# Attention weights times values in high and low parts, two query blocks at a time

## The chip, the core and the metric

The kernel runs on one core of a Trainium2 chip. The metric is the device time of one execution in microseconds; the median of repeated runs is compared. The core has a matrix engine, TensorE (PE in the rows; PEld is its load of the stationary operand), three engines for elementwise work, VectorE (DVE), ScalarE (ACT) and GpSimd (POOL), and SyncE (SP), which issues DMAs. SBUF is the working memory of 128 partitions, PSUM the memory that TensorE writes, in banks of 512 fp32 columns.

## The reference

One layer of a hybrid block over 1024 prompt tokens and 8 decode tokens of width 1024: differential attention with 8 heads and a gated linear recurrence with 8 heads side by side, then a convolutional feed-forward part. The change touches the attention of the prompt alone, and of it the last product:

```python
s = jnp.einsum('bqhcd,bkhcd->bhcqk', qi, k).astype(F32) * scale
s = jnp.where(kpos[None, :] <= qpos[:, None], s, -jnp.inf)
p = diff_probs(s, lam)        # softmax(s)[c=0] - lam * softmax(s)[c=1]
return jnp.einsum('bhqk,bkhv->bqhv', p.astype(v.dtype), v)
```

Queries go in 8 blocks of 128; block i sees the keys of blocks 0 to i. Everything is fp32.

## The kernel before

The work is laid out by hand: each engine has its own program, and semaphores (`Sig`) order them. The stages are a norm stage, the heads stage, a gates stage and the tail with the feed-forward part. The change is in `heads_stage`, which takes the first half of the span. There a loop over the heads h = 0 to 7 does three things at once: the attention of head h, its recurrence, and the large projections of the inputs (`piece(h, n)`, 21 pieces of 24 products in a head, helper `product` at L170). A piece multiplies high and low parts of weights and of activations: three products of type float32r (high by high, high by low, low by high) for each of 8 contraction tiles, 344 columns wide. Plain fp32 products are also used; in the trace each of those is two MATMUL records, each float32r product is one.

The attention of a head goes through eight query blocks i = 0 to 7 (in the texts: block 0 to 7). For a block, in the order of the data:

- `scores_of(h, i)` on TensorE (L1038): queries times keys into PSUM (`h_S`).
- `maxima(h, i)` on VectorE (L1332 to L1336): mask, row maxima.
- two exponentials on ScalarE (L903) into `E` (`h_a_E`), with their sums.
- `weigh(h, i)` on VectorE (L1342 to L1347): the weights, which raises `weighed`.
- the transposes on TensorE (L1090), i + 1 of them, into the PSUM tile `Xf` (`h_X`), which raises `turned`.
- a copy on ScalarE from `Xf` to `PT` in SBUF (L929), which raises `pt_ready`.
- `values(i, n)` on TensorE (L1067): i + 1 plain fp32 products of 128 columns, `vtok` (the values, tokens on partitions, copied from PSUM at L911) by `PT`, summed in a bank of `G` beside the bank of the next piece; then `read_values(i)` on ScalarE (L897) copies the bank to `oraw`.

TensorE's own program in block i is: scores of block i + 1 (for i + 1 below 4), one piece (i below 4) or two pieces, `values(i - 1)`, in blocks 1 and 2 of heads 1 to 7 a sum matmul for the norm of the recurrence of the head before (`o_sum`, L1049), the transposes of block i, then the scores of block i + 1 (for i + 1 from 4 on). After block 7 come eight transposes of another input, the piece `FILL_PIECE`, `values(7)`, and then the eight chunks of the recurrence, each with a piece among its products. ScalarE's program in blocks 1 and 2 takes the sum's reciprocal root (`o_norm`, L887 and L889) ahead of its copy of the transposes, and VectorE applies it (L1418, L1422) ahead of the next `weigh`.

## Time and profile before

| | us |
|---|---|
| median of 3 runs | 2320.13 |
| lowest and highest | 2319.94 and 2320.91 |
| span of the profiled execution | 2317.6 |
| TensorE busy in it | 2283.8 |
| VectorE busy | 1433.6 |
| ScalarE busy | 1046.8 |
| GpSimd busy | 805.3 |

The span runs from the first to the last instruction of one profiled execution; a run's time holds a little more, what lies around it. A record of a matmul is drawn from its start to the modelled end of its last result, and the next one starts before that end. So the distance from one start to the next tells what a matmul costs, and the length of a record does not. The granted clock of TensorE was 0.997 of full speed (2.4 GHz) over the span. A time in the timeline is counted from the start of the span.

### The profile page before, as it was taken

How to read it: one execution, taken by the hardware profiler on the slowest of the kernel's cores; microseconds unless marked ns; L12 is line 12 of the kernel's file. 1: busy time of each engine (PE TensorE's matmuls, PEld its weight loads, DVE VectorE, ACT ScalarE, POOL GpSimd, SP SyncE). 2: the span in 40 equal slices, each digit the busy share in tenths (PEclk: the TensorE clock that was granted, in tenths of full speed). 3: DMA queues.
4: the chain of work that ended last, by engine and by line, in shares of the span. 5: the costliest groups of instructions: out<-in, count | busy, mean ns of one | idle time of the engine just before them, and what ended most of it. 6: DMA issues, size and time to landing. Idle time of an engine off the chain costs nothing. (4 is left out here: it accounts for less than half of the span.)

```text
span 2317.6 us, 46133 instructions
## 1 busy us (share of the span) xinstructions
PE 2283.8 (99%) x18425; PEld 2153.4 (93%) x18425; DVE 1433.6 (62%) x2594; ACT 1046.8 (45%) x2114; POOL 805.3 (35%) x1019
## 2 busy tenths in 40 slices
PE   7999999999999999999999999999999999999999
PEld 5898989989898989899888999999999999999999
DVE  5667676777676776765787324337546545555557
ACT  6656656556566656564333321125333333332331
POOL 1143342626252434424444124442222323222222
PEclk9999999999999999999999999999999999999999
DMA  7213121222312131211899413111111111111113
GB/s 299 92 47 103 41 87 59 73 77 57 102 54 95 49 101 49 92 46 53 326 346 347 159 61 104 46 48 51 46 46 46 46 46 46 54 43 51 46 46 99
DMA packets 75057, 213.19 MB, mean 92 GB/s; under 512 B 15579, under 2 KB 23643, under 8 KB 74843
## 3 DMA queue, kind: packets, MB, share of 16 engines
q1 hardware_dynamic: 73690, 206.05, 26.6%
q10 hardware_dynamic: 1152, 4.19, 0.4%
q8 instruction: 146, 2.39, 0.4%
q14 instruction: 69, 0.56, 0.1%
HBM read 175.49 MB, written 26.26 MB: 87 GB/s over the span
## 5 line engine op out<-in xcount | busy, mean ns | idle before, releaser
L170 PE MATMUL h_G<-xn_hi,h_w_hi 128*128 128x344 f32 x1368 | 457.7, 335 | 0.2 <-ACT h_d_oraw L897 0.2
L170 PE MATMUL h_G<-xn_hi,h_w_lo 128*128 128x344 f32 x1368 | 437.1, 319 | 0.0
L170 PE MATMUL h_G<-xn_lo,h_w_hi 128*128 128x344 f32 x1368 | 436.5, 319 | 0.0
L2419 POOL TENSOR_TENSOR h_w_lo<-h_w_raw,h_w_hi 128x1024 fp32r<-128x1024 f32 x87 | 215.7, 2480 | 488.8 <-DVE f_y L2620 208.7
L2341 PE MATMUL t_ps<-hn_hi,h_w_hi 128*128 128x344 f32 x1024 | 327.7, 320 | 0.9 <-issue 0.9
L2341 PE MATMUL t_ps<-hn_lo,h_w_hi 128*128 128x344 f32 x1024 | 327.1, 319 | 0.0
L2341 PE MATMUL t_ps<-hn_hi,h_w_lo 128*128 128x344 f32 x1024 | 327.0, 319 | 0.0
L1167 POOL TENSOR_TENSOR h_w_lo<-h_w_raw,h_w_hi 128x1024 fp32r<-128x1024 f32 x58 | 149.2, 2572 | 432.6 <-ACT h_w_hi L764 365.0
L170 PEld LDWEIGHTS h_G<-xn_hi,h_w_hi 128*128 128x128 f32 x1368 | 258.4, 189 | 32.5 <-issue 21.5
L170 PEld LDWEIGHTS h_G<-xn_lo,h_w_hi 128*128 128x128 f32 x1368 | 257.1, 188 | 4.4 <-issue 0.2
L170 PEld LDWEIGHTS h_G<-xn_hi,h_w_lo 128*128 128x128 f32 x1368 | 257.1, 188 | 0.0
L2199 ACT ACTIVATE f_u<-t_ps 128x344 f32<-128x344 f32 x132 | 59.9, 459 | 336.5 <-PE t_ps L2341 335.5
L2149 ACT ACTIVATE h_w_hi<-h_w_raw 128x1024 fp32r<-128x1024 f32 x87 | 91.5, 1053 | 266.5 <-PE t_ps L170 256.5
L2341 PEld LDWEIGHTS t_ps<-hn_hi,h_w_hi 128*128 128x128 f32 x1024 | 192.3, 188 | 1.4 <-issue 1.4
L2341 PEld LDWEIGHTS t_ps<-hn_hi,h_w_lo 128*128 128x128 f32 x1024 | 192.5, 188 | 0.0
L2341 PEld LDWEIGHTS t_ps<-hn_lo,h_w_hi 128*128 128x128 f32 x1024 | 192.3, 188 | 0.0
L2505 DVE SCALAR_TENSOR_TENSOR x<-t_ps,keep_mod,x 128x344 f32<-128x344 f32 (+1 forms) x288 | 149.5, 564 | 68.4 <-PE t_ps L170 67.6
L2613 DVE TENSOR_SCALAR f_y<-f_old,keep_vec 128x8 f32<-128x8 f32 x44 | 16.2, 369 | 259.8 <-ACT f_u L2199 259.8
L170 PE MATMUL t_ps<-f_act_hi,h_w_hi 128*128 128x344 f32 x528 | 169.8, 322 | 0.0
L170 PE MATMUL t_ps<-f_act_hi,h_w_lo 128*128 128x344 f32 x528 | 169.0, 320 | 0.0
L170 PE MATMUL t_ps<-f_act_lo,h_w_hi 128*128 128x344 f32 x528 | 168.7, 320 | 0.0
L903 ACT ACTIVATE h_a_E<-h_S,h_d_sm 128x256 f32<-128x256 f32 (+7 forms) x128 | 93.6, 738 | 115.1 <-DVE h_d_sm L1336 115.1
(403 smaller groups left out, 5510.3 us busy)
## 6 DMA issues: line engine op xcount, KB each, us to landing
h_w_raw<-in_w_in SPq DMA_DIRECT2D x72, 512.0 KB, 3.8
h_w_raw<-in_w_ffn SPq DMA_DIRECT2D x66, 512.0 KB, 3.6
h_d_ada_w<-in_w_ada SPq DMA_DIRECT2D x32, 512.0 KB, 4.3
g_kp<-in_cache_k SPq DMA_DIRECT2D x32, 512.0 KB, 7.1
g_vp<-in_cache_v SPq DMA_DIRECT2D x32, 512.0 KB, 5.6
h_w_raw<-in_w_mix SPq DMA_DIRECT2D x24, 512.0 KB, 3.6
x<-in_xT SPq DMA_DIRECT2D x16, 516.0 KB, 7.5
n_ada_w<-in_w_ada SPq DMA_DIRECT2D x16, 512.0 KB, 13.8
```

The costliest lines, as they stand in the source:

```text
L170: ins = eng.matmul(out, w[:, k * P:(k + 1) * P], x[:, k, columns], start=(k == 0 and n == 0), stop=(k == n_k - 1 and n == 2))
L903: ins = act.activation(E[:, m, 0:nk], SP_[:, :, :].rearrange("p a b -> p (a b)")[:, 512 * score_bank(i, m):512 * score_bank(i, m) + nk], A ...
L1167: pool.tensor_tensor(wlo[w][:, :], raw[r][:, :], whi[w][:, :].bitcast(F32), ALU.subtract).then_inc(lo_done.sem, 1)
L2149: act.activation(whi[buf(n)][:, :], raw[n % 2][:, :], ACT.Copy).then_inc(w_hi.sem, 1)
L2199: act.activation(u[s][:, 2 + j * TH:2 + (j + 1) * TH], ffn_bank(t, 0, j), ACT.Copy).then_inc(up_free.sem, 1)
L2341: ins = pe.matmul(ffn_bank(t, 0, j), wp[w][:, k * P:(k + 1) * P], xp[:, k, cols(j)], start=(k == 0 and q == 0), stop=(k == KT - 1 and q == 2))
L2419: pool.tensor_tensor(wlo[buf(n)][:, :], raw[n % 2][:, :], whi[buf(n)][:, :].bitcast(F32), ALU.subtract).then_inc(w_lo.sem, 1)
L2505: ins = dve.scalar_tensor_tensor(out=xt[:, a0:a0 + n], in0=bank[:, 0:n], scalar=gain[:, 0:1], in1=xt[:, a0:a0 + n], op0=ALU.mult, op1=ALU.add)
L2613: ch(dve.tensor_scalar(ys[:, T:NT], st[0], w[0], w[3], ALU.mult, ALU.add))
```

## The change

The values and the transposed weights are each kept as a high part (float32r, rounded on the copy out of PSUM by ScalarE) and a low part (the difference of PSUM and high part, a subtraction on VectorE). `values(j, n)` now treats the two query blocks 2j and 2j + 1 together: for each of 2j + 2 key blocks three float32r products, high values by high weights, high by low, low by high, 256 columns wide; the last key block is seen by the second query block only, and its three are 128 wide. It is called in blocks 2, 4 and 6 and after `FILL_PIECE`, and one copy of 256 columns reads its bank. `low_values` (one subtraction) and `low_weights` (one or two) are new in VectorE's program. The transposes of a block now wait until high and low weights of the block before have been taken from `Xf`. Buffers change places to make room: `pt_hi` lies over the buffers of the rotation, part of which moves to the place of `E`; the low values lie over the second buffer of the adaptive weights, so its load now waits in SyncE's queue for the last products (`pv_done`), ahead of `turn_piece(h, 1)`.

```diff
         qT, kT, vT = (mem(n, [P, NT]) for n in ("qT", "kT", "vT"))
-        vtok = mem("vtok", [P, T])
+        v_at = mem.off
+        v_hi = mem("vtok_hi", [P, T], F32R)
         kk, fc, qh, ib, og = (mem(n, [P, NT]) for n in ("kk", "fc", "qh", "ib", "og"))
         ibtok = mem("ibtok", [P, T])
         AT, kht, St, subg = mem("AT", [P, P]), mem("kht", [P, P]), mem("St", [P, P]), mem("subg", [P, 1])
...
         LK = [mem(f"LK{i}", [P, LEVELS, P]) for i in range(2)]
-        LQ = [mem(f"LQ{i}", [P, LEVELS + 1, P]) for i in range(2)]
+        LQ = [mem("LQ0", [P, LEVELS + 1, P])]
+        pt_lo = [None, Memory(nc, "h_lq", mem.off)("pt_low1", [P, T], F32R)]
+        LQ.append(mem("LQ1", [P, LEVELS + 1, P]))
         braw = mem("braw", [P, T])
         ex = [mem(f"ex{i}", [P, TH]) for i in range(2)]
         PT = Memory(nc, "h_c", R3 + WIDE)("PT", [P, T])
+        v_first = Memory(nc, "h_vt", v_at)("vtok_first", [P, T])
+        pt_lo[0] = Memory(nc, "h_pt", R3 + WIDE)("pt_low0", [P, T], F32R)
         mem = Memory(nc, "h_d", R3 + WIDE + ROW, early["lmask_at"])
-        rg = [mem(f"rg{i}", [P, TH]) for i in range(2)]
-        rt = [mem(f"rt{i}", [P, TH]) for i in range(2)]
-        rows = Memory(nc, "h_rows", mem.off)("rows", [H * NS, 2, P])
-        sq = [mem(f"sq{i}", [P, TH]) for i in range(2)]
+        pt_at = mem.off
+        pt_hi = Memory(nc, "h_turn", pt_at)("pt_high", [P, NB, 2, P], F32R)
+        rest = Memory(nc, "h_rest", R3, R3 + 2 * ROW)
+        rg, rt, sq = ([rest(f"{n}0", [P, TH]), mem(f"{n}1", [P, TH])] for n in ("rg", "rt", "sq"))
+        rows = mem("rows", [H * NS, 2, P])
+        mem.off = pt_at + NB * 2 * P * 4
         oraw = mem("oraw", [P, T])
+        v_lo = Memory(nc, "h_aw", mem.off + KT * P * 4)("vtok_lo", [P, T], F32R)
         aw, av = [mem(f"ada_w{i}", [P, KT * P]) for i in range(2)], [mem(f"ada{i}", [P, P]) for i in range(2)]
         sm = mem("sm", [P, 16])
         dec, neg_mid = mem("dec", [P, NB]), mem("neg_mid", [P, NB])
...
 
-        def value_bank(i):
-
-            return (ATT_PIECES[i + 1][-1] + 1) % 2 if i + 1 < NB else (FILL_PIECE + 1) % 2
+        def value_bank(j):
+
+            return (ATT_PIECES[2 * j + 2][-1] + 1) % 2 if 2 * j + 2 < NB else (FILL_PIECE + 1) % 2
+
+        def pt_low(b):
+
+            at = b % (NB // 2) * 2 * P
+            return pt_lo[b // (NB // 2)][:, at:at + 2 * P]
+
+        def low_half(n, i, blocks):
+
+            return pt_lo[n][:, :].rearrange("p (b q t) -> p b q t", q=2, t=P)[:, 0:blocks, i % 2, :]
 
 
         def sum_bank(h, u):
...
-                        load_ada(h, 1, 0)
                     if t == 4 and h:
                         store_branch(h - 1, 2)
                         store_branch(h - 1, 3)
                     if t == NTL:
                         turn_piece(h, 0)
                     load(t)
+                sp.wait_ge(pv_done.sem, pv_done.at(h, NB // 2))
+                load_ada(h, 1, 0)
                 turn_piece(h, 1)
                 load_ada(h, 2, 14)
...
 
-                def read_values(i):
-                    act.wait_ge(pv_done.sem, pv_done.at(h, i + 1))
-                    if i == 0 and h:
+                def read_values(j):
+                    act.wait_ge(pv_done.sem, pv_done.at(h, j + 1))
+                    if j == 0 and h:
                         act.wait_ge(a_stored.sem, a_stored.at(h, 0))
-                    act.activation(oraw[:, i * P:(i + 1) * P], G[:, value_bank(i), 0:P], ACT.Copy).then_inc(pv_read.sem, 1)
+                    act.activation(oraw[:, 2 * j * P:2 * (j + 1) * P], G[:, value_bank(j), 0:2 * P], ACT.Copy).then_inc(pv_read.sem, 1)
 
                 for i in range(NB):
                     nk = (i + 1) * P
...
-                        act.activation(vtok[:, :], Xf, ACT.Copy).then_inc(v_tok.sem, 1)
+                        act.activation(v_hi[:, :], Xf, ACT.Copy).then_inc(v_high.sem, 1)
                     for n in ATT_PIECES[i]:
                         if n != READ_FIRST:
                             split_next(h, n)
                         piece(h, n)
                         if n == READ_FIRST:
                             split_next(h, n)
-                    if 0 < i:
-                        read_values(i - 1)
+                    if i in (2, 4, 6):
+                        read_values(i // 2 - 1)
                     if i in (1, 2) and h:
                         o_norm(h - 1, i + 1)
                     if i == 4:
...
-                read_values(NB - 1)
+                read_values(NB // 2 - 1)
                 sigmoid(h, len(SIGMOID) - 1)
 
                 for k in range(NB):
...
                 pe.wait_ge(st_ready.sem, st_ready.at(h, 0))
 
-                def values(i, n):
-
-                    pe.wait_ge(pt_ready.sem, pt_ready.at(h, i + 1))
+                def values(j, n):
+
+                    pe.wait_ge(pt_high.sem, pt_high.at(h, 2 * j + 2))
+                    pe.wait_ge(pt_lowed.sem, pt_lowed.at(h, 2 * j + 2))
                     pe.wait_ge(piece_read.sem, piece_read.at(h, n))
-                    for b in range(i + 1):
-                        ins = pe.matmul(G[:, value_bank(i), 0:P], vtok[:, b * P:(b + 1) * P], PT[:, b * P:(b + 1) * P],
-                                        start=(b == 0), stop=(b == i))
+                    for b in range(2 * j + 2):
+                        q = slice(0 if b <= 2 * j else P, 2 * P)
+                        high = pt_hi[:, b, :, :].rearrange("p q t -> p (q t)")[:, q]
+                        low, out, at = pt_low(b)[:, q], G[:, value_bank(j), q], slice(b * P, (b + 1) * P)
+                        pe.matmul(out, v_hi[:, at], high, start=(b == 0), stop=False)
+                        pe.matmul(out, v_hi[:, at], low, start=False, stop=False)
+                        ins = pe.matmul(out, v_lo[:, at], high, start=False, stop=(b == 2 * j + 1))
                     ins.then_inc(pv_done.sem, 1)
 
                 for i in range(NB):
                     if i + 1 < NB // 2:
                         scores_of(h, i + 1)
                     for n in ATT_PIECES[i]:
-                        if n == ATT_PIECES[i][0] and i >= 2:
-                            pe.wait_ge(pv_read.sem, pv_read.at(h, i - 1))
+                        if n == ATT_PIECES[i][0] and i in (3, 5, 7):
+                            pe.wait_ge(pv_read.sem, pv_read.at(h, (i - 1) // 2))
                         piece(h, n)
-                    if 0 < i:
-                        values(i - 1, ATT_PIECES[i][-1])
+                    if i in (2, 4, 6):
+                        values(i // 2 - 1, ATT_PIECES[i][-1])
                     if i in (1, 2) and h:
                         if i == 2:
                             pe.wait_ge(o_rstd.sem, o_rstd.at(h - 1, 3))
@@ -1085,7 +1109,11 @@
                         pe.wait_ge(o_rstd.sem, o_rstd.at(h, 0))
                     pe.wait_ge(weighed.sem, weighed.at(h, i + 1))
                     if i == 0:
-                        pe.wait_ge(v_tok.sem, v_tok.at(h, 1))
+                        pe.wait_ge(v_high.sem, v_high.at(h, 1))
+                        pe.wait_ge(v_low.sem, v_low.at(h, 1))
+                    else:
+                        pe.wait_ge(pt_high.sem, pt_high.at(h, i))
+                        pe.wait_ge(pt_lowed.sem, pt_lowed.at(h, i))
                     for b in range(i + 1):
                         ins = pe.transpose(Xf[:, b * P:(b + 1) * P], E[:, 0, b * P:(b + 1) * P], ident[:, :])
                     ins.then_inc(turned.sem, 1)
...
                         scores_of(h, i + 1)
                 pe.wait_ge(piece_read.sem, piece_read.at(h, 9))
                 turn8(Sf, ib).then_inc(ib_turned.sem, 1)
-                pe.wait_ge(pv_read.sem, pv_read.at(h, NB - 1))
                 piece(h, FILL_PIECE)
-                values(NB - 1, FILL_PIECE)
+                values(NB // 2 - 1, FILL_PIECE)
                 for k in range(NB):
                     ck = slice(k * P, (k + 1) * P)
                     pe.wait_ge(lv_k.sem, lv_k.at(h, k + 1))
...
+
+            def low_values(h):
+
+                dve.wait_ge(v_high.sem, v_high.at(h, 1))
+                if h:
+                    dve.wait_ge(ada_read.sem, ada_read.at(h, 0))
+                dve.tensor_tensor(v_lo[:, :], Xf, v_hi[:, :].bitcast(F32), ALU.subtract).then_inc(v_low.sem, 1)
+
+            def low_weights(h, i):
+
+                dve.wait_ge(pt_high.sem, pt_high.at(h, i + 1))
+                for n in range(1 + i // (NB // 2)):
+                    at = n * NB // 2
+                    blocks = min(NB // 2, i + 1 - at)
+                    ins = dve.tensor_tensor(low_half(n, i, blocks), Xf[:, at * P:(at + blocks) * P].rearrange("p (b t) -> p b t", t=P),
+                                            pt_hi[:, at:at + blocks, i % 2, :].bitcast(F32), ALU.subtract)
+                ins.then_inc(pt_lowed.sem, 1)
...
                 for i in range(NB):
                     weigh(h, i)
+                    if i == 0:
+                        low_values(h)
...
                         o_norm(h - 1, i + 1)
                     if NB // 2 <= i + 1 < NB:
                         maxima(h, i + 1)
+                    low_weights(h, i)
```

TensorE, second head: the end of a piece, the products of block 1 and the transposes of block 2, before. `h_c_PT` are the transposed weights, `h_vtok` the values, `h_d_rstd_o` what the sum matmul sums, `h_a_E` the weights.

```order
L170 MATMUL h_G<-xn_hi,h_w_lo_79 128x344
L1067 MATMUL h_G<-h_c_PT,h_vtok 128x128 [waits h_piece_read,h_pt_ready]
L1067 MATMUL h_G<-h_c_PT,h_vtok 128x128
L1049 MATMUL h_X<-h_d_rstd_o,keep_ones_50 128x512 [waits h_o_squared,h_o_rstd]
L1090 MATMUL h_X<-keep_ident,h_a_E 128x128 [waits h_weighed]
L1090 MATMUL h_X<-keep_ident,h_a_E 128x128 x2
L170 MATMUL h_G<-xn_hi,h_w_hi_78 128x344 [waits h_w_lo_done,h_piece_read,h_w_hi_done,h_pv_read]
```

The same place with the change (`h_turn_pt_high` and `h_pt_pt_low` are the high and low weights, `h_vtok_hi` and `h_aw_vtok_lo` the values):

```order
L170 MATMUL h_G<-xn_hi,h_w_lo_79 128x344
L1090 MATMUL h_G<-h_turn_pt_high,h_vtok_hi 128x256 [waits h_piece_read,h_pt_low,h_pt_high]
L1091 MATMUL h_G<-h_pt_pt_low_827,h_vtok_hi 128x256
L1092 MATMUL h_G<-h_turn_pt_high,h_aw_vtok_lo 128x256
L1090 MATMUL h_G<-h_turn_pt_high,h_vtok_hi 128x128
L1091 MATMUL h_G<-h_pt_pt_low_827,h_vtok_hi 128x128
L1092 MATMUL h_G<-h_turn_pt_high,h_aw_vtok_lo 128x128
L1068 MATMUL h_X<-h_d_rstd_o,keep_ones_50 128x512 [waits h_o_squared,h_o_rstd]
L1118 MATMUL h_X<-keep_ident,h_a_E 128x128 [waits h_pt_low,h_pt_high,h_weighed]
L1118 MATMUL h_X<-keep_ident,h_a_E 128x128 x2
L170 MATMUL h_G<-xn_hi,h_w_hi_78 128x344 [waits h_w_lo_done,h_piece_read,h_w_hi_done,h_pv_read]
```

Two products of 128 columns have become six of up to 256, for blocks 0 and 1 together, and the transposes wait for two more semaphores.

TensorE, second head, the end of block 3's piece and the transposes of block 3, before:

```order
L170 MATMUL h_G<-xn_lo,h_w_hi_78 128x344
L170 MATMUL h_G<-xn_hi,h_w_lo_80 128x344
L1067 MATMUL h_G<-h_c_PT,h_vtok 128x128 [waits h_piece_read,h_pt_ready]
L1067 MATMUL h_G<-h_c_PT,h_vtok 128x128 x2
L1090 MATMUL h_X<-keep_ident,h_a_E 128x128 [waits h_weighed]
L1090 MATMUL h_X<-keep_ident,h_a_E 128x128 x3
L1038 MATMUL h_S<-h_kT,h_qT 128x512
```

and with the change:

```order
L170 MATMUL h_G<-xn_lo,h_w_hi_78 128x344
L170 MATMUL h_G<-xn_hi,h_w_lo_80 128x344
L1118 MATMUL h_X<-keep_ident,h_a_E 128x128 [waits h_pt_low,h_pt_high,h_weighed]
L1118 MATMUL h_X<-keep_ident,h_a_E 128x128 x3
L1057 MATMUL h_S<-h_kT,h_qT 128x512
L1057 MATMUL h_S<-h_kT,h_qT 128x128
```

Nothing stands any more between the piece and the transposes.

VectorE, second head, between the row maxima and the weights of block 3, before (`h_b_braw` and `h_og` are of the norm, L1342 is the reciprocal with which `weigh` starts):

```order
L1363 TENSOR_SCALAR h_fc<-h_b_ex_823,keep_lb 128x344 [waits h_sig_ready]
L1365 TENSOR_SCALAR h_kk<-h_fc 128x344 [waits h_dve_chain]
L1418 SCALAR_TENSOR_TENSOR h_b_braw<-h_b_braw,keep_vec,h_d_rstd_o 128x512 [waits h_o_rstd]
L1422 TENSOR_TENSOR h_b_braw<-h_b_braw,h_og 128x512 [waits h_dve_chain]
L1342 RECIPROCAL h_d_sm<-h_d_sm 128x2 [waits h_exped]
L1344 TENSOR_TENSOR h_d_sm<-h_d_sm,keep_lam 128x1 [waits h_dve_chain]
L1345 TENSOR_SCALAR h_a_E<-h_a_E,h_d_sm 128x512
```

and with the change:

```order
L1407 TENSOR_SCALAR h_fc<-h_b_ex_824,keep_lb 128x344 [waits h_sig_ready]
L1409 TENSOR_SCALAR h_kk<-h_fc 128x344 [waits h_dve_chain]
L1462 SCALAR_TENSOR_TENSOR h_b_braw<-h_b_braw,keep_vec,h_d_rstd_o 128x512 [waits h_o_rstd]
L1466 TENSOR_TENSOR h_b_braw<-h_b_braw,h_og 128x512 [waits h_dve_chain]
L1390 TENSOR_TENSOR h_pt_pt_low_827<-h_X,h_turn_pt_high 128x3x128 [waits h_pt_high]
L1369 RECIPROCAL h_d_sm<-h_d_sm 128x2 [waits h_exped]
L1371 TENSOR_TENSOR h_d_sm<-h_d_sm,keep_lam 128x1 [waits h_dve_chain]
L1372 TENSOR_SCALAR h_a_E<-h_a_E,h_d_sm 128x512
```

The subtraction for the low weights of block 2 (L1390, three blocks of 128) has come in ahead of the reciprocal of block 3.

## Rows read from the trace of the kernel before

**Rows 1.** The page: its first line and busy time by engine

```profile
span 2317.6 us, 46133 instructions
...
PE 2283.8 (99%) x18425; PEld 2153.4 (93%) x18425; DVE 1433.6 (62%) x2594; ACT 1046.8 (45%) x2114; POOL 805.3 (35%) x1019
```

**Rows 2.** Groups of TensorE by line and form: records, busy us, mean ns, idle before

```profile
L1067 PE MATMUL h_G<-h_c_PT,h_vtok 128*128 128x128 f32 x576 | 74.6, 275 | 0.0
```

**Rows 3.** Timeline of TensorE, blocks 2 and 3: start us, length us, instruction, records

```profile
603.25 0.61 PE L1067 MATMUL h_G<-h_c_PT,h_vtok 128*128 128x128 f32 x4
603.70 1.02 PE L1049 MATMUL h_X<-h_d_rstd_o,keep_ones 128*128 128x512 f32 x2
604.56 0.49 PE L1090 MATMUL h_X<-keep_ident,h_a_E 128*128 128x128 f32 x3
604.80 0.41 PE L170 MATMUL h_G<-xn_hi,h_w_hi 128*128 128x344 f32 x1
605.05 0.32 PE L170 MATMUL h_G<-xn_lo,h_w_hi 128*128 128x344 f32 x1
...
608.65 0.83 PE L1067 MATMUL h_G<-h_c_PT,h_vtok 128*128 128x128 f32 x6
609.46 0.66 PE L1090 MATMUL h_X<-keep_ident,h_a_E 128*128 128x128 f32 x4
```

**Rows 4.** Timeline of TensorE at two records of nine columns

```profile
585.05 0.28 PE L1019 MATMUL h_G<-keep_pick,h_d_ada 128*128 128x9 f32 x2
585.19 0.47 PE L1150 MATMUL h_S<-h_AT,h_ibtok 128*128 128x128 f32 x2
585.49 0.39 PE L1152 MATMUL h_S<-h_b_LQ,h_St 128*128 128x128 f32 x2
```

**Rows 5.** Timeline of ScalarE up to the exponentials of block 3

```profile
604.76 0.69 ACT L887 ACTIVATE h_d_rstd_o<-h_X,keep_eps 128x512 f32<-128x512 f32 x1 [0.45 <-PE h_X L1049]
...
606.02 0.47 ACT L929 ACTIVATE h_c_PT<-h_X 128x384 f32<-128x384 f32 x1
606.39 0.68 ACT L903 ACTIVATE h_a_E<-h_S,h_d_sm 128x512 f32<-128x512 f32 x1
...
607.05 0.69 ACT L903 ACTIVATE h_a_E<-h_S,h_d_sm 128x512 f32<-128x512 f32 x1
```

**Rows 6.** Timeline of VectorE up to the weights of block 3

```profile
606.93 0.69 DVE L1422 TENSOR_TENSOR h_b_braw<-h_b_braw,h_og 128x512 f32<-128x512 f32 x1
607.86 0.17 DVE L1342 RECIPROCAL h_d_sm<-h_d_sm 128x2 f32<-128x2 f32 x1 [0.23 <-ACT h_a_E L903]
...
608.65 0.75 DVE L1347 SCALAR_TENSOR_TENSOR h_a_E<-h_a_E,h_d_sm 128x512 f32<-128x512 f32 x1
```

**Rows 7.** Timeline of VectorE: ends of weighing in blocks 5 and 7

```profile
627.45 1.02 DVE L1347 SCALAR_TENSOR_TENSOR h_a_E<-h_a_E,h_d_sm 128x768 f32<-128x768 f32 x1
...
650.49 0.17 DVE L1342 RECIPROCAL h_d_sm<-h_d_sm 128x2 f32<-128x2 f32 x1 [2.37 <-ACT h_a_E L903]
...
651.54 1.28 DVE L1347 SCALAR_TENSOR_TENSOR h_a_E<-h_a_E,h_d_sm 128x1024 f32<-128x1024 f32 x1
```

**Rows 8.** Timeline of TensorE: products and transposes of blocks 5 and 7

```profile
629.68 1.27 PE L1067 MATMUL h_G<-h_c_PT,h_vtok 128*128 128x128 f32 x10
630.79 0.82 PE L1090 MATMUL h_X<-keep_ident,h_a_E 128*128 128x128 f32 x6
...
652.69 1.72 PE L1067 MATMUL h_G<-h_c_PT,h_vtok 128*128 128x128 f32 x14
654.25 1.04 PE L1090 MATMUL h_X<-keep_ident,h_a_E 128*128 128x128 f32 x8
```

**Rows 9.** Timelines: first transposes of two heads, the values' copy, a long product

```profile
465.16 0.27 PE L1090 MATMUL h_X<-keep_ident,h_a_E 128*128 128x128 f32 x1
...
589.29 1.02 ACT L911 ACTIVATE h_vtok<-h_X 128x1024 f32<-128x1024 f32 x1
...
591.99 0.27 PE L1090 MATMUL h_X<-keep_ident,h_a_E 128*128 128x128 f32 x1
...
642.40 1.22 DVE L1445 TENSOR_TENSOR h_fc<-h_fc,h_qh 128x1024 f32<-128x1024 f32 x1
```

More of the change, by code:

```diff
@@ L604, in heads_stage @@
         scores, row_max, exped, weighed = S("scores", 8), S("row_max", 8), S("exped", 8), S("weighed", 8)
-        turned, pt_ready, pv_done, pv_read = S("turned", 8), S("pt_ready", 8), S("pv_done", 8), S("pv_read", 8)
-        v_turned, v_tok = S("v_turned", 1), S("v_tok", 1)
+        turned, pv_done, pv_read = S("turned", 8), S("pv_done", 4), S("pv_read", 4)
+        pt_high, pt_lowed = S("pt_high", 8), S("pt_low", 8)
+        v_turned, v_high, v_low = S("v_turned", 1), S("v_high", 1), S("v_low", 1)
         ib_turned, ib_tok = S("ib_turned", 1, init=1), S("ib_tok", 1)
@@ L620, in heads_stage @@
         wt = a["w_in"]
-        spare = [E[:, :, :].rearrange("p a b -> p (a b)"), PT[:, :], oraw[:, :], braw[:, :], vtok[:, :]]
+        spare = [E[:, :, :].rearrange("p a b -> p (a b)"), PT[:, :], oraw[:, :], braw[:, :], v_first[:, :]]
         first_pair = [spare[0][:, 0:2 * TH], spare[0][:, 2 * TH:4 * TH], spare[1][:, 0:2 * TH]]
@@ L1119, in _ @@
                     if k == 0:
-                        pe.wait_ge(pv_read.sem, pv_read.at(h, NB))
+                        pe.wait_ge(pv_read.sem, pv_read.at(h, NB // 2))
                     if REC_PIECES[k][0] in ADA_AT:
```

6 lines of the change are left out of this document (3 added, 3 removed).

## The prediction

> **What bounds the kernel now.** I read the page first: over a span of 2317.6 us the matmul row of TensorE is busy 2283.8 us, 99% [rows 1]. Work taken off TensorE should then come off the span one for one. But a busy row only says that the records touch each other, since each is drawn longer than the distance to the next one. So the second view is the timeline of TensorE, read by starts: what a group costs is the start of the next group less its own start, and a wait shows only as a group that costs more than its count of records. Third, the timelines of VectorE and ScalarE around the places where TensorE needs their result. I use the fifth head (h = 4, 586 to 662 us) as the pattern of heads 1 to 7; each has the same groups at the same distances.
>
> The weights times values are 576 records on L1067 [rows 2]: 36 products in each of 8 heads, two records to a product. Fourteen of them take 654.25 - 652.69 = 1.56 us [rows 8], 111.4 ns each; I write 112. A head spends 72 x 112 = 8.06 us on them, all heads 64.5 us. TensorE also waits once in a head: in block 3 six records should take 0.67 us and take 609.46 - 608.65 = 0.81 us [rows 3], because the weights of block 3 are finished only at 608.65 + 0.75 = 609.40 [rows 6]. The transposes start 0.06 us later. That wait of 0.14 us says that block 3 has no slack at all. This is the view that the forecast hangs on.
>
> **The new products.** A head now has 60 instead of 36: for the pairs of query blocks 6, 12, 18 and 24; of these 48 are 256 columns wide and 12 are 128. No product of this type at these widths is in the trace. The nearest row is the same type at 344 columns: 23 of them in 608.65 - 605.05 = 3.60 us, 156.5 ns each [rows 3]. From above, a 256-column product costs no more than that. From below stands the load of a new stationary tile: four records, two with only 9 moving columns and two with 128, take 585.49 - 585.05 = 0.44 us, 110 ns each [rows 4], so a narrow record is not cheaper, and about 112 ns is what a change of stationary tile costs. In proportion to columns 344 to 256 gives 156.5 x 256 / 344 = 116.5 ns; I take 117, nearer to the floor of 112, and 112 for the 128-column ones. A head's products are then 48 x 117 + 12 x 112 = 6.96 us instead of 8.06: **1.10 us less**, 8.8 us in all. Ends for the 256s: 107 ns (two passes over 512 columns took 0.43 us a record, 0.42 ns a column [rows 3]) gives another 3.8 us, 157 ns takes back 15 us.
>
> The Trainium skill (TensorE: Matmul & The Clock Gate, Back-to-back issue gap) gives a warm gap of columns / 2.4 + 2.5 ns. For 344 columns this is 146 ns and the trace has 156.5; for a record of 9 columns it gives 6 ns, against 110 in [rows 4]. The same page (LDWEIGHTS) puts a load at columns / 1.2, 107 ns, and the trace agrees with that one. By the first formula the new products would take 47 us in all instead of 56; that case is a rival below.
>
> **Where the products stand.** Before, block i - 1's products stood ahead of the transposes of block i, and so covered the wait for block i's weights. Now pairs stand ahead of the transposes of blocks 2, 4 and 6 and after the last block; ahead of 1, 3, 5 and 7 stands nothing. Block by block (before, then after, in us; where no row is named, a count of records by 0.112):
> Block 1: 0.22, then 0. The sum matmul still covers it.
> Block 2: 0.45 (4 records), then 6 products, 0.69.
> Block 3: 0.81, then only waiting. In heads 1 to 7 the chain starts at the end of the sum matmul (604.56): ScalarE takes its logarithm at 604.76, then exponentials, the copy at 606.02, the scores' exponentials from 606.39 to 607.74 [rows 5], VectorE from 607.86 to 609.40 [rows 6]. That is 4.90 us to the transposes' start, while the work of TensorE left in between is 608.65 - 604.56 = 4.09 us [rows 3]. The wait is 0.81 us: the products leave and the time stays. VectorE also gets the subtraction of the low weights of block 2 ahead of the reciprocal. It is 384 elements; 512 took 0.69 us [rows 6] and 1024 took 1.22 [rows 9], so about 0.56, and 0.47 from start to start. VectorE is free for 0.23 us there (607.62 to 607.86 [rows 6]), so the chain gets some 0.25 us longer (bounds 0 and 0.35). Block 3 then costs 1.06.
> Block 4: 0.90, then 12 products, 1.39. Weights are ready long before.
> Block 5: 1.11 (630.79 - 629.68), then 0: the weights are ready at 627.45 + 1.02 = 628.47 and TensorE would come at 629.68 [rows 7, 8], 1.2 us to spare. A true gain.
> Block 6: 1.34, then 18 products, 2.09.
> Block 7: 1.56, then a wait: TensorE would come at 652.69, the weights are ready at 651.54 + 1.28 = 652.82 [rows 7, 8], so 0.19 with the 0.06 of handing over.
> After the last block: 1.79, then 24 products, 2.79.
> Sum before 0.22 + 0.45 + 0.81 + 0.90 + 1.11 + 1.34 + 1.56 + 1.79 = 8.18, after 0.69 + 1.06 + 1.39 + 2.09 + 0.19 + 2.79 = 8.21. **Per head the change moves this sum by 0.03 us, that is by nothing.** The 1.10 us of work goes into 0.25 + 0.67 us at block 3 and 0.19 us at block 7.
> In the first head no sum matmul starts block 3's chain, and I count its gain there as kept: 1.10 - 0.19, about 0.9 us.
>
> **What else moves.** VectorE gets 13 more instructions a head, some 6.7 us beside its 62% [rows 1]. For blocks 3 to 6 they stand after the row maxima, where VectorE idles until the exponentials come (2.37 us at block 7 [rows 7], against at most 0.69 + 0.56 us): nothing. The subtraction for the last block stands ahead of the first operands of the recurrence, beneath a piece of 3.8 us on TensorE: nothing; without that cover 1.2 us a head. The low values: the high copy ends at 589.29 + 1.02 = 590.31, plus 1.22 is 591.6, and TensorE comes to its first transposes at 591.99 [rows 9]: covered with 0.4 us left; the maxima of block 1 move behind it, which the next exponentials just allow. Behind TensorE's new waits on the low parts is its whole queue, but each of these parts is due more than 1 us before. ScalarE reads four double banks instead of eight, less work off the path; the bank of a pair is read while TensorE transposes. SyncE now holds the second adaptive-weight load until the last product, with one exchange of rotated rows queued behind it, which waits for a later piece anyway; the load is used two pieces on, some 12 us later: nothing, or a few tenths were it late. Buffers that only change places cost nothing.
>
> **The sum.** Seven heads at +0.03 and one at -0.9 are about -0.7 us; which makes 2317.6 - 0.7 = 2316.9 us of span. The median of the runs, 2320.13, is 2.5 us over the span; so the forecast is **2319.4 us**.
>
> **Rivals.**
> Faster, the page's reading: TensorE sets the end and the chain of block 3 does not last, because the copies and sums ahead of it move earlier. The whole 8.8 us come off: 2311.3. For it: 99% busy. Against it: 0.06 us between weights and transposes at block 3, and a chain that starts from TensorE's own sum matmul, which moves with it. 10%.
> Faster, columns alone: weight loads hide fully, a 256 costs 107 ns and a 128 costs 54: 384 x 107 + 96 x 54 = 46.3 us, 18.2 less than 64.5, 9.4 more than mine: about 2310. [Rows 4] speak against it. This is what the formula of the skill above amounts to. 7%.
> Slower, narrow products: if the single pass is not granted at 128 columns, each of the 96 costs what a full product costs now, 224 ns: 96 x 112 = 10.8 us, none of it covered since they stand in the groups of blocks 2, 4, 6 and at the end: 2330. It decides from 160 ns on (4.6 us). Nothing in the trace excludes it. 10%.
> Slower, VectorE's queue: the low values come later than 0.4 us at the head's start, or the low weights hit block 3 harder than 0.35 us; 0.6 us a head more brings 2324.5 and above. 8%.
> That it does not do what it says (products still in two records each) would be the narrow case for all 480: + 50 us; 1%.
>
> **How the numbers follow.** The forecast has 64%. Within it the 256-column pitch (112 to 124 ns) moves the sum by -1.9 to +2.7 us and the delay at block 3 by another 2. A measurement of this kernel tells about 0.2%, 4.6 us, from no change. Faster 0.17, same 0.64, slower 0.19. The range takes in the edge of the faster cases and most of the slower one: 2311 to 2327.
>
> **What would show it.** In the new trace: 6, 12, 18, 24 records a group, 117 ns apart (112 if narrow); transposes of block 3 starting 5.1 us after the sum matmul, 0.06 us after the weights, with 1 us of idleness or a stretched last piece before them; those of block 7 likewise with 0.2; block 5 with none. A head from first transposes to first transposes stays at 591.99 - 465.16 = 126.8 us [rows 9]. Wrong is the forecast if that distance is shorter by 1 us (chain gone) or if a 128-column product is 200 ns.

## The result and the profile after

The changed kernel takes 2345.23 us (median of 4 runs, 2344.69 to 2348.25); the kernel before, run beside it, 2320.52 us (2319.94 to 2322.41). The ratio is 1.0109, with a 95% interval of 1.0094 to 1.0123: about 25 us slower, where 2319.4 us and at most 2327 had been forecast. The times here and below are medians; one run of the fourth experiment's control, which took 2777.62 us at a granted clock of 0.752, is left out of them.

The first lines of the page of the changed kernel (span; busy us, share and instructions by engine), beside [rows 1]:

```profile
span 2342.9 us, 46020 instructions
...
PE 2284.7 (98%) x18329; PEld 2146.5 (92%) x18329; DVE 1501.4 (64%) x2698; ACT 1042.3 (44%) x2082; POOL 800.4 (34%) x1019
```

TensorE's busy time is the same to 1 us, and the span has grown by 25.3 us: by this row the time is not work of TensorE. From the first transposes of head 3 to those of head 4 the kernel before takes 126.8 us and the changed one 129.1. The starts of the transposes (L1090 before, L1118 after) cut head 3 into steps; "step 2 to 3" runs from the first transpose of query block 2 to that of block 3:

| step | before | after | change | the forecast's change |
|---|---|---|---|---|
| block 0 to 1 | 6.01 | 5.78 | -0.23 | -0.22 |
| 1 to 2 | 6.56 | 6.89 | +0.33 | +0.24 |
| 2 to 3 | 4.90 | 6.09 | **+1.19** | +0.25 |
| 3 to 4 | 10.42 | 10.88 | +0.46 | +0.49 |
| 4 to 5 | 10.90 | 9.82 | -1.08 | -1.11 |
| 5 to 6 | 11.46 | 12.19 | +0.73 | +0.75 |
| 6 to 7 | 12.00 | 10.67 | -1.33 | -1.37 |
| 7 to next head | 64.58 | 66.77 | **+2.19** | +1.00 |
| head | 126.83 | 129.09 | +2.26 | +0.03 |

Six of eight steps came out within 0.1 us. Two did not.

**Block 3.** TensorE's timeline of head 4 in the changed kernel (start us, length us, line, instruction, records; in brackets the idle time before it and who ended it) answers to [rows 3]:

```profile
614.04 0.28 PE L1090 MATMUL h_G<-h_turn_pt_high,h_vtok_hi 128*128 128x256 f32 x1
614.16 0.28 PE L1091 MATMUL h_G<-h_pt_pt_low,h_vtok_hi 128*128 128x256 f32 x1
614.27 0.28 PE L1092 MATMUL h_G<-h_turn_pt_high,h_aw_vtok_lo 128*128 128x256 f32 x1
614.39 0.23 PE L1090 MATMUL h_G<-h_turn_pt_high,h_vtok_hi 128*128 128x128 f32 x1
614.45 0.27 PE L1091 MATMUL h_G<-h_pt_pt_low,h_vtok_hi 128*128 128x128 f32 x1
614.56 0.28 PE L1092 MATMUL h_G<-h_turn_pt_high,h_aw_vtok_lo 128*128 128x128 f32 x1
614.68 1.07 PE L1068 MATMUL h_X<-h_d_rstd_o,keep_ones 128*128 128x512 f32 x2
615.67 0.55 PE L1118 MATMUL h_X<-keep_ident,h_a_E 128*128 128x128 f32 x3
...
621.76 0.66 PE L1118 MATMUL h_X<-keep_ident,h_a_E 128*128 128x128 f32 x4 [1.79 <-DVE h_a_E L1374]
622.35 2.35 PE L1057 MATMUL h_S<-h_kT,h_qT 64*128 64x512 f32 x8
```

The new products are there as forecast (starts 0.12 us apart), and the transposes of block 3 wait 1.79 us of plain idleness for VectorE's L1374, the last instruction of the weighing. The cause stands one block earlier. GpSimd's subtraction there (L1167 before, L1194 after) makes the low part of a tile of projection weights, `h_w_lo`; ScalarE's high part and this low part together are the split of a tile, and `SPLIT_AT` says before which piece each split is made. VectorE and GpSimd in the changed kernel, while block 2 is weighed:

```profile
611.76 0.42 DVE L1390 TENSOR_TENSOR h_pt_pt_low<-h_X,h_turn_pt_high 128x256 fp32r<-128x256 f32 x1
612.10 0.16 DVE L1369 RECIPROCAL h_d_sm<-h_d_sm 128x2 f32<-128x2 f32 x1
...
612.37 0.42 DVE L1372 TENSOR_SCALAR h_a_E<-h_a_E,h_d_sm 128x384 f32<-128x384 f32 x1
612.82 2.80 DVE L1374 SCALAR_TENSOR_TENSOR h_a_E<-h_a_E,h_d_sm 128x384 f32<-128x384 f32 x1
615.53 0.42 DVE L1359 TENSOR_TENSOR h_S<-h_S,h_causal 128x256 f32<-128x256 f32 x1
```

```profile
612.81 2.38 POOL L1194 TENSOR_TENSOR h_w_lo<-h_w_raw,h_w_hi 128x1024 fp32r<-128x1024 f32 x1 [4.38 <-issue]
```

The same in the kernel before (VectorE, then GpSimd):

```profile
601.71 0.62 DVE L1347 SCALAR_TENSOR_TENSOR h_a_E<-h_a_E,h_d_sm 128x384 f32<-128x384 f32 x1
602.24 0.43 DVE L1332 TENSOR_TENSOR h_S<-h_S,h_causal 128x256 f32<-128x256 f32 x1
```

```profile
602.02 2.54 POOL L1167 TENSOR_TENSOR h_w_lo<-h_w_raw,h_w_hi 128x1024 fp32r<-128x1024 f32 x1 [4.61 <-issue]
```

One instruction of one shape takes 0.62 us where it starts 0.31 us ahead of GpSimd's subtraction, and 2.80 us where it starts 0.01 us behind it; it ends 0.43 us after GpSimd does. In between stands the new subtraction L1390 (0.42 us), the low part of block 1's weights, which pushed the weighing back. Everything behind it on VectorE is 2.2 us later: the maxima of block 3 (615.53), the norm, the low part and the weighing of block 3.

**Piece 12.** The end of the head in the changed kernel, on TensorE and on GpSimd:

```profile
666.91 1.09 PE L1118 MATMUL h_X<-keep_ident,h_a_E 128*128 128x128 f32 x8
667.84 1.04 PE L1063 MATMUL h_S<-keep_ident,h_ib 128*128 128x128 f32 x8
669.85 0.40 PE L170 MATMUL h_G<-xn_hi,h_w_hi 128*128 128x344 f32 x1 [0.97 <-issue]
```

```profile
667.14 2.60 POOL L1194 TENSOR_TENSOR h_w_lo<-h_w_raw,h_w_hi 128x1024 fp32r<-128x1024 f32 x1 [16.68 <-ACT h_w_hi L783]
```

Piece 12 needs the low part of its weights, and GpSimd writes it until 669.74. TensorE follows 0.11 us later. In the kernel before it was a near thing already:

```profile
655.13 1.04 PE L1044 MATMUL h_S<-keep_ident,h_ib 128*128 128x128 f32 x8
655.99 0.39 PE L170 MATMUL h_G<-xn_hi,h_w_hi 128*128 128x344 f32 x1
```

```profile
653.13 2.61 POOL L1167 TENSOR_TENSOR h_w_lo<-h_w_raw,h_w_hi 128x1024 fp32r<-128x1024 f32 x1 [17.03 <-ACT h_w_hi L764]
```

655.74 against 655.99: a quarter of a microsecond to spare, behind fourteen products (1.56 us) that have now left block 7. The column on the idle time names nobody ("issue"), since TensorE's wait is for two semaphores; GpSimd's end tells which one it was.

**Clock.** In heads 2, 4 and 7 TensorE's granted clock falls to 1.2 GHz for 3.4 us behind the wait of block 3. Stretches of the changed kernel at about the same place of heads 3 and 4 (busy us of each engine and instructions, then the granted clock, the DMA share and GB/s):

```profile
493.70:497.10 3.40, 3.40 (x24) 2.95 (x21) 2.35 (x4) 0.49 (x2) 0.00 (x0) 1.00 0.02 5
622.60:626.00 3.40, 3.40 (x13) 2.19 (x12) 1.32 (x3) 0.46 (x1) 0.00 (x0) 0.50 0.02 5
```

At a clock of 0.50 TensorE does 13 records where it else does 24. The step from block 3 to block 4 takes 12.47 us in head 4 instead of 10.88: 1.55 to 1.6 us in each of three heads. The kernel before has no such stretch in its heads (it has some outside them, and so has every version).

**The account.** Seven heads at +2.3 us are 16; three clock stretches 4.7; head 0 +1.7 (the same two waits); the start, before the first head, +0.9 (the first matmul is already 0.56 us later, before any of the changed work); the stages behind the last head about +1.8. Together 25 us.

### The profile page after: what moved, and what is told of

Read it like the earlier page. It is cut to its first block and busy times, and to the rows that moved or that the text cites. A ratio compares the mean times of both kernels' runs of the same rounds, so it can differ in the third digit from the quotient of the medians.

```text
span 2342.9 us, 46020 instructions
## 1 busy us (share of the span) xinstructions
PE 2284.7 (98%) x18329; PEld 2146.5 (92%) x18329; DVE 1501.4 (64%) x2698; ACT 1042.3 (44%) x2082; POOL 800.4 (34%) x1019
## 3 DMA queue, kind: packets, MB, share of 16 engines
q8 instruction: 145, 2.38, 0.4%
## 5 line engine op out<-in xcount | busy, mean ns | idle before, releaser
L1194 POOL TENSOR_TENSOR h_w_lo<-h_w_raw,h_w_hi 128x1024 fp32r<-128x1024 f32 x58 | 148.0, 2552 | 448.9 <-ACT h_w_hi L783 369.3
```

Of the source, the lines that this page charges most:

```text
L1194: pool.tensor_tensor(wlo[w][:, :], raw[r][:, :], whi[w][:, :].bitcast(F32), ALU.subtract).then_inc(lo_done.sem, 1)
```

## The experiments

**First: take each suspected wait away by an edit of order alone.** The low part of block 1 goes behind the weighing of block 2:

```diff
                 for i in range(NB):
                     weigh(h, i)
+                    if i == 2:
+                        low_weights(h, 1)
...
-                    low_weights(h, i)
+                    if i != 1:
+                        low_weights(h, i)
```

> The changed kernel with one subtraction moved: VectorE makes the low part of query block 1's weights behind the weighing of block 2 instead of ahead of it. The same work is done. Theory A (the 0.42 us subtraction pushes the last instruction of weigh(2), 128x384, into GpSimd's split of the values' projection weights, 612.81 to 615.19 us in the profile, where it takes 2.80 us instead of the 0.62 us of before, and everything behind it on VectorE is late): the instruction takes about 0.6 us again, the transposes of block 3 start some 5.15 us after those of block 2 instead of 6.09, and the three stretches at half TensorE clock (heads 2, 4 and 7) are gone. 7 x 0.94 = 6.6 us and 3 x 1.55 = 4.65 us: about 2334 us, where the changed kernel has 2345. Rival (VectorE simply has 0.42 us more to do in front of block 3, wherever it stands): no gain, 2345 us, block 3 waits as long as now. Second rival (the instruction is slow for its operands' new places in memory): it keeps its 2.8 us.

Measured: 2333.17 us, ratio to before 1.0050 (1.0033 to 1.0067). The profiled run is the slowest of the four (2338.86 us), with more stretches at 1.2 GHz outside the heads; its heads are read here. VectorE and GpSimd:

```profile
608.05 0.62 DVE L1374 SCALAR_TENSOR_TENSOR h_a_E<-h_a_E,h_d_sm 128x384 f32<-128x384 f32 x1
608.59 0.42 DVE L1390 TENSOR_TENSOR h_pt_pt_low<-h_X,h_turn_pt_high 128x256 fp32r<-128x256 f32 x1
```

```profile
608.37 2.55 POOL L1194 TENSOR_TENSOR h_w_lo<-h_w_raw,h_w_hi 128x1024 fp32r<-128x1024 f32 x1 [4.38 <-issue]
```

0.62 us in all eight heads; block 3 starts 5.04 us after block 2, no stretch at 1.2 GHz is left in the heads. Theory A was right to 1 us, and both rivals fall: the same instructions with the same operands cost 12 us less.

The split of the tile for piece 12, one piece earlier:

```diff
-SPLIT_AT = {1: 1, 2: 6, 4: 2, 7: 3, 10: 4, 12: 5, 19: 7}
+SPLIT_AT = {1: 1, 2: 6, 4: 2, 7: 3, 9: 4, 12: 5, 19: 7}
```

> The changed kernel with the split of the tile for piece 12 made at piece 9 instead of piece 10 (ScalarE's high part and GpSimd's low part, both), so ahead of the exponentials of block 7 on ScalarE. Nothing else is changed. Theory B (since products left block 7, TensorE reaches piece 12 before GpSimd's 2.6 us subtraction has ended, and waits 1.14 us a head for it): piece 12 follows the turns of ib without a wait, 8 x 1.14 = 9 us less, about 2336 us. Rival (the wait hides another one, for example the split colliding with VectorE's weighing of block 6 or making ScalarE late in block 6): less than 4 us are gained, and the wait shows up at the transposes of block 6 or 7.

Measured: 2332.82 us, ratio 1.0054 (1.0037 to 1.0071). Piece 12 follows the turns of ib without a wait:

```profile
662.57 1.04 PE L1063 MATMUL h_S<-keep_ident,h_ib 128*128 128x128 f32 x8
663.36 0.41 PE L170 MATMUL h_G<-xn_hi,h_w_hi 128*128 128x344 f32 x1
```

A head takes 127.85 us where the clock holds, 1.2 less than in the changed kernel. It gained 12.4 us, not 9: eight times 1.2 are 9.7, the profiled run has two stretches at 1.2 GHz in its heads (1 and 2) instead of three, which is 1.6, and 1 us I cannot place. No new wait came up at blocks 6 or 7. Theory B holds.

Both edits in one kernel:

```diff
                     weigh(h, i)
+                    if i == 2:
+                        low_weights(h, 1)
...
-                    low_weights(h, i)
+                    if i != 1:
+                        low_weights(h, i)
...
-SPLIT_AT = {1: 1, 2: 6, 4: 2, 7: 3, 10: 4, 12: 5, 19: 7}
+SPLIT_AT = {1: 1, 2: 6, 4: 2, 7: 3, 9: 4, 12: 5, 19: 7}
```

> Both edits in one: the low part of block 1's weights behind the weighing of block 2, and the split for piece 12 at piece 9. If the two causes are separate, their gains add up: 11 + 9 = 20 us below the changed kernel, about 2325 us. The kernel before has 2320.5; what is then still missing, about 4 us, is the longer wait at block 3 (7 x 0.25), the start before the heads (0.9) and head 0. Rival (they are one cause, seen twice): the sum is no better than the better of the two, about 2334.

Measured: 2323.65 us (10 runs), ratio 1.0016 (1.0007 to 1.0026). The gains add up, to 21.6 us (12.1 and 12.4 us singly; both took away stretches at 1.2 GHz). A head takes 126.7 to 126.9 us, as in the kernel before, and against the kernel before its steps in head 3, in the order of the table above, are -0.23, +0.24, +0.14, +0.46, -1.08, +0.72, -1.33 and +0.97 us. What was forecast for the change is what it does once both hidden waits are gone.

**Second: put the cause of A into the kernel before**, with its old products, by an instruction that nobody needs:

```diff
                 for i in range(NB):
+                    if i == 2:
+                        ch(dve.tensor_reduce(sm[:, 12:13], cos[:, 0:300], AX.X, ALU.max))
                     weigh(h, i)
```

> The kernel before (its products as they were) with one instruction more: VectorE takes a maximum over 300 columns of a constant table, some 0.35 to 0.4 us, ahead of the weighing of block 2, and nobody reads it. Theory A (a delay of about 0.4 us at this place is all that it takes, since the last instruction of weigh(2) then starts after GpSimd's subtraction has): that instruction takes 2.5 to 2.8 us instead of 0.62, block 3 waits 1 us a head longer, 8 us and perhaps some stretches at half clock on top: 2328 to 2333 us. Rival (the products' new form or the buffers are the cause): 0.4 us is hidden or at most added, 2320.5 to 2323.5 us, and the instruction stays at 0.6 us.

Measured: 2328.21 us, ratio 1.0029 (1.0017 to 1.0041). A head takes 127.6 to 128.0 us, 1.0 to 1.2 more than before: the step to block 2 is 0.32 longer and the step to block 3 0.73. VectorE, GpSimd in head 4:

```profile
606.78 0.46 DVE L1429 TENSOR_REDUCE h_d_sm<-h_cos 128x1 f32<-128x300 f32 x1
...
607.87 2.75 DVE L1347 SCALAR_TENSOR_TENSOR h_a_E<-h_a_E,h_d_sm 128x384 f32<-128x384 f32 x1
```

```profile
607.83 2.37 POOL L1167 TENSOR_TENSOR h_w_lo<-h_w_raw,h_w_hi 128x1024 fp32r<-128x1024 f32 x1 [4.61 <-issue]
```

and in head 0, where the two start the other way round:

```profile
97.68 0.62 DVE L1347 SCALAR_TENSOR_TENSOR h_a_E<-h_a_E,h_d_sm 128x384 f32<-128x384 f32 x1
```

```profile
97.73 2.82 POOL L1167 TENSOR_TENSOR h_w_lo<-h_w_raw,h_w_hi 128x1024 fp32r<-128x1024 f32 x1 [3.02 <-issue]
```

In seven heads VectorE starts 0.04 us behind GpSimd and takes 2.75 us; in head 0 it starts 0.05 us ahead and takes 0.62. 7.4 us for some 0.36 us of delay a head, none of it in the products: A needs nothing of the change but the delay. No head of this run has a stretch at 1.2 GHz.

**Third: take GpSimd away instead, and leave VectorE's order.** The changed kernel, with the split of the values' projection weights at piece 3:

```diff
-SPLIT_AT = {1: 1, 2: 6, 4: 2, 7: 3, 10: 4, 12: 5, 19: 7}
+SPLIT_AT = {1: 1, 3: 6, 4: 2, 7: 3, 10: 4, 12: 5, 19: 7}
```

> The changed kernel, VectorE's order left as it is, but the split of the values' projection weights (ScalarE's high part and GpSimd's low part) made at piece 3 instead of piece 2, so that GpSimd is idle while block 2 is weighed. Theory A (it is GpSimd's subtraction, running from the same moment, that holds the last instruction of weigh(2) for 2.8 us; VectorE's 0.42 us alone do nothing): the instruction takes 0.62 us with the low part of block 1 still ahead of it, block 3 starts about 5.1 us after block 2, the stretches at half clock go: 2345 - 11 = 2334 us, if ScalarE's high part, some 1.2 us, finds room in block 3 (if not, it lies in block 3's chain, and 7 us are lost again: 2341). Rival (VectorE's place in its own queue is the cause): 2.8 us and 2345 us.

Measured: 2330.49 us, ratio 1.0048 (1.0034 to 1.0063); 15 us below the changed kernel. Its heads take 128.0 us, as those of the first experiment (127.9); the other 2.7 us lie outside the heads and are not explained. L1374 takes 0.62 us in all heads with L1390 still ahead of it, and block 3 starts 5.04 us after block 2. So it is the coincidence of the two, and removing either side removes it. GpSimd now runs during block 3 (613.98 to 616.83), and holds another instruction there:

```profile
615.12 1.90 DVE L1397 TENSOR_SCALAR h_b_ex<-h_b_ex 128x344 f32<-128x344 f32 x1 [0.50 <-ACT h_b_ex L850]
```

Its like take 0.33 us. Little on the path waits for it here: the step to block 4 is 10.97 us instead of 10.88.

**Fourth: is the change worth something without the chain of block 3?** On top of the first two edits (low part and split for piece 12), the norm of the head before is moved behind the exponentials (ScalarE) and behind the weighing (VectorE) of blocks 2 and 3:

```diff
                     ins.then_inc(exped.sem, 1)
+                    if i in (2, 3) and h:
+                        o_norm(h - 1, i)
...
-                    if i in (1, 2) and h:
-                        o_norm(h - 1, i + 1)
...
                     weigh(h, i)
+                    if i in (2, 3) and h:
+                        o_norm(h - 1, i)
...
-                    if i in (1, 2) and h:
-                        o_norm(h - 1, i + 1)
```

> Three edits in the changed kernel: the low part of block 1 behind weigh(2), the split for piece 12 at piece 9, and the norm of the head before (ScalarE's logarithm and exponential, VectorE's two products) behind the exponentials and the weighing of blocks 2 and 3 instead of ahead of them. Theory C (with the first two edits the changed kernel lacks a gain only since block 3 waits 0.95 us a head for a chain that starts at TensorE's sum matmul and runs over that norm; TensorE has the 8 us less work that the change was credited with): the wait of 0.95 us goes in seven heads, 2323.65 - 6.7 = 2317 us, 0.1 to 0.2% below the kernel before; a head takes 125.8 us from first transposes to first transposes. Rival (something else in block 3, the copy of the turned weights or the scores' exponentials, is just as late): less than 2 us gained, 2322 us or more.

Measured: 2315.86 us (11 runs), ratio 0.9982 (0.9973 to 0.9990), the fastest of all. ScalarE turns to the copy and the exponentials of block 3 at once, and TensorE's transposes follow the piece without idleness:

```profile
604.78 0.49 ACT L948 ACTIVATE h_turn_pt_high<-h_X 128x384 fp32r<-128x384 f32 x1 [0.85 <-PE h_X L1118]
605.17 0.68 ACT L922 ACTIVATE h_a_E<-h_S,h_d_sm 128x512 f32<-128x512 f32 x1
...
606.49 0.70 ACT L906 ACTIVATE h_d_rstd_o<-h_X,keep_eps 128x512 f32<-128x512 f32 x1
```

```profile
608.21 0.32 PE L170 MATMUL h_G<-xn_hi,h_w_lo 128*128 128x344 f32 x1
608.36 0.60 PE L1118 MATMUL h_X<-keep_ident,h_a_E 128*128 128x128 f32 x4
```

Block 3 starts 4.11 us after block 2, with 0.17 us between weights and transposes; a head takes 125.71 us, 0.9 to 1.1 less than before. How much of that the products bring, and how much the order alone, a control has to tell.

The control is the kernel before with the same two moves of the norm and the earlier split:

```diff
-SPLIT_AT = {1: 1, 2: 6, 4: 2, 7: 3, 10: 4, 12: 5, 19: 7}
+SPLIT_AT = {1: 1, 2: 6, 4: 2, 7: 3, 9: 4, 12: 5, 19: 7}
...
+                    if i in (2, 3) and h:
+                        o_norm(h - 1, i)
...
-                    if i in (1, 2) and h:
-                        o_norm(h - 1, i + 1)
```

> The kernel before with the two edits that exist for it: the split for piece 12 at piece 9, and the norm of the head before behind the exponentials and the weighing of blocks 2 and 3. Its products are as they were. Theory C (in the kernel before the products of block 2 fill block 3's wait but for 0.14 us, and the split has 0.25 us to spare): 0 to 1 us less, 2320 to 2321 us, and the two versions differ by the products. Rival (the orders are better whatever the products are): 4 us less or more, 2316 us or below.

Measured: 2319.45 us (10 runs), ratio 0.9991 (0.9982 to 1.0000). A head takes 126.4 us, 0.3 less than before on average: 0.14 from block 3, 0.05 from the step behind it, 0.06 to 0.08 from piece 12, and in some heads 0.19 at a later chunk of the recurrence. So a third of the gain of the version above belongs to the order, and the new products bring 0.67 us a head in the traces. They are themselves 1.27 us shorter (48 times 118 ns and 12 times 95 on average, against 8.06 us). Of the rest, 0.2 stays in the wait of block 7, and 0.23 more in the step from the first to the second chunk of the recurrence, before which TensorE idles 0.35 us instead of 0.15; the last 0.15 I have not placed. In the times the difference is near the noise: the medians differ by 3.6 us, the runs reach from 2313.32 to 2319.94 and from 2316.56 to 2322.59, and the intervals of the two ratios overlap.

The last one is the fastest version (with the norm's moves) with GpSimd moved in place of the low part, which stands where the change had put it:

```diff
-SPLIT_AT = {1: 1, 2: 6, 4: 2, 7: 3, 10: 4, 12: 5, 19: 7}
+SPLIT_AT = {1: 1, 3: 6, 4: 2, 7: 3, 9: 4, 12: 5, 19: 7}
```

> The changed kernel with the split of the values' weights at piece 3 in place of the moved low part, and the other two edits (split for piece 12 at piece 9, the norm behind the exponentials and the weighing). By theories A and C it should come to the same 2317 us as the version with the low part moved, if ScalarE has room for 1.2 us in block 3; the norm of the head before now stands there as well, so ScalarE may be late for block 4: up to 1 us a head, 2325 us, as the rival has it.

Measured: 2326.92 us, ratio 1.0028 (1.0016 to 1.0040): the rival's side. Block 3 is as early as in the fastest version, but the step from block 3 to block 4 has grown from 10.83 to 12.28 us in head 4:

```profile
614.75 0.69 DVE L1466 TENSOR_TENSOR h_b_braw<-h_b_braw,h_og 128x512 f32<-128x512 f32 x1
615.94 1.94 DVE L1397 TENSOR_SCALAR h_b_ex<-h_b_ex 128x344 f32<-128x344 f32 x1 [0.50 <-ACT h_b_ex L850]
617.80 0.45 DVE L1407 TENSOR_SCALAR h_fc<-h_b_ex,keep_lb 128x344 f32<-128x344 f32 x1
```

```profile
614.80 2.89 POOL L1194 TENSOR_TENSOR h_w_lo<-h_w_raw,h_w_hi 128x1024 fp32r<-128x1024 f32 x1 [11.84 <-ACT h_w_hi L783]
```

Counted from the start of block 3's transposes, L1397 starts at 1.72 us instead of the 1.14 of the fastest version, since ScalarE, with its part of the split to do, hands over later (0.58 us). Then it takes 1.94 us instead of 0.33, and ends 0.19 us after GpSimd's subtraction (617.69); that is 1.61 us more. The maxima of block 4 stand behind it. So both of the split's halves lie in the chain, and GpSimd's is the larger part; whether ScalarE's alone would cost anything no run shows. The exponentials of block 4 then start at 620.74, the split that follows them on ScalarE at 622.29, and the reading of piece 5's bank last:

```profile
625.08 0.36 PE L1090 MATMUL h_G<-h_turn_pt_high,h_vtok_hi 128*128 128x256 f32 x1 [1.22 <-ACT h_qh L856]
```

The collision was only moved from block 2 to block 3. In the third experiment, where L1397 is held as well, it cost 0.1 us a head, since block 3 itself came 0.93 us later there; here it costs 1.45.

## Why the prediction was wrong

**The durations held.** 256 columns take 118 ns (117 forecast). Of the 128-column products the first takes 60 ns and the next two 111 and 113, so 95 on average instead of 112 (the forecast's floor of 112 ns for any width did not hold for the first). The rival of narrow products at 224 ns falls. Of the table's steps five came within 0.05 us, the gain of block 5 and the wait of block 7 among them, and the step to block 2 within 0.1.

**Block 3 was mis-sized: "the chain gets some 0.25 us longer (bounds 0 and 0.35)"; it got 1.19 us.** The failed step is the price of VectorE's new instructions: the prediction took each at its own length and gave the low part of block 1, ahead of weigh(2), no term at all. The mechanism was the one foreseen for another place, a low part that is queued ahead of a weighing. The prediction looked at the low part of block 2, ahead of weigh(3), which behaved (+0.14 us in the run with both edits). For weigh(2) it might have named the slack on TensorE's side, 2.23 us between weights and transposes. That slack was real and was eaten whole, since 0.42 us of delay became 0.42 + 2.2 by GpSimd. What had to be asked was not only who waits for weigh(2) but what runs beside it. The trace of before showed the effect, in each of its eight heads. In block 4 L1353 (128x344, both sides in SBUF) takes 2.00 us beside GpSimd's subtraction and ends 0.19 us after it, where 3.4 us later it takes 0.34:

```profile
617.55 2.00 DVE L1353 TENSOR_SCALAR h_b_ex<-h_b_ex 128x344 f32<-128x344 f32 x1 [0.45 <-ACT h_b_ex L831]
620.98 0.34 DVE L1353 TENSOR_SCALAR h_b_ex<-h_b_ex 128x344 f32<-128x344 f32 x1 [1.00 <-ACT h_b_ex L831]
```

```profile
616.40 2.96 POOL L1167 TENSOR_TENSOR h_w_lo<-h_w_raw,h_w_hi 128x1024 fp32r<-128x1024 f32 x1 [11.84 <-ACT h_w_hi L764]
```

And in block 2 itself a 128x2 instruction takes 0.63 us, ending with GpSimd's subtraction (604.56), where at 591.48 it takes 0.17:

```profile
603.96 0.63 DVE L1336 TENSOR_SCALAR h_d_sm<-h_d_sm 128x2 f32<-128x2 f32 x1
```

The slower rival had the mechanism's name ("the low weights hit block 3 harder than 0.35 us"; 8%), not its cause, nor its size of 7 x 0.94 = 6.6 us and the clock on top.

The Trainium skill (GPSIMD Engine Reference, Specifications) states this contention: GpSimd shares its SBUF interfaces with VectorE, and VectorE's instructions that have two SBUF inputs or run in a two-port mode contend with it. The traces agree: held were L1374 (two inputs in SBUF; 2.80 us for 0.62) and L1397 (one input in SBUF, one output; 1.94 for 0.33; that it runs in the mode named no trace shows), while the mask addition and the maximum with their input in PSUM ran at their normal 0.43 and 1.22 us beside GpSimd. Both ended 0.2 to 0.4 us after GpSimd's subtraction did, so they were held until about its end.

**"After the last block: 1.79, then 24 products, 2.79" left out what stands ahead of them.** This is the second failed step, a wait that the sum does not have. The products of block 7 had covered GpSimd's subtraction for piece 12 to within 0.25 us. With 1.56 us of products gone and 0.19 us of waiting in their place, TensorE arrives 1.1 us too early. In the step table this is 2.19 instead of 1.00. The prediction checked the cover of each wait that the edit touched in the code, and this one is not in the edit. It also named no wait for the pieces' own weights anywhere. Eight times 1.14 us (from the turn of ib to piece 12 it now takes 1.25 us instead of 0.11) is 9.1 us.

**The first head** was counted at -0.9 us and came at +1.7: both waits are there as well (its L1374 took 2.73 us). With both edits it still gains only 0.3 (124.84 us against 125.17), since TensorE then idles 0.5 us ahead of its block 7, which the prediction did not have.

**The clock** was not in the sum at all: 3 x 1.55 us. Within the heads it fell only in the two versions in which TensorE idles 1.76 to 1.79 us before block 3 (three heads of the changed kernel, two of the run with the earlier split), and in none of those in which it idles 0.8 us or less there. With the same idleness the other nine heads of the two versions had no fall.

**The start and the later stages** differ between the profiled runs of the versions, mostly to the slow side of the kernel before: by -0.1 to +3.7 us up to the first transposes, and by +0.8 to +3.7 us (in the first experiment's run, the slowest of its kernel, +8.1) behind the heads. The five runs that are more than 2 us late at the first transposes all have a stretch of 3.4 us at 1.2 GHz at 57 to 59 us, which the others lack. Why it comes there I have not explained.

**What was right** was the core of the argument: the products' gain does not reach the end, because block 3 hangs on a chain and not on TensorE. With both waits removed a head takes 126.7 to 126.9 us, as forecast (126.8), and the 2323.65 us are within the forecast's range, 4 us above its middle. In the profiled run TensorE is done with the heads at the same time as before (it starts the next stage at 1104.24 us, before at 1104.37); the 3.7 us more lie behind them, in stages that the change does not touch. With the chain cut as well, a part of the gain appears (0.7 us a head against the control).

## What to carry to other kernels

When an edit adds or delays work on VectorE, lay GpSimd's long instructions beside VectorE's timeline and look at what will now start just behind one: an instruction of the kinds that were held here (wide inputs in SBUF) then costs GpSimd's remaining time and a little more, not its own length. Instructions of one line and shape that take different times in the trace of before are the sign to look for. When an edit takes work from the engine that sets the pace, list every semaphore that this engine waits for behind that work, those of untouched code too, and write down the slack of each; 0.25 us of slack under 1.4 us of removed work is a new wait. An edit that measures as a loss may still be right: first repair the two places where it ran into others, then judge it.
